# First mixer on x as it lands, with a third pair of output weights and zero products ahead; 106 filler instructions taken out

## The chip, the cores and the metric

One core of one Trainium2 chip runs the whole program. The metric is the device time of one execution in microseconds. The median over the runs shown is 1749.64 us for the kernel before.

## What is computed

The reference runs four layers over one sequence of 256 tokens with 1024 channels, all in float32: an even mixer, a retention mixer, a pool mixer and an MLA attention, each followed by a feed-forward part (a gated convolutional one in the first two layers, a mixture of 32 experts in the last two). The change is to the first, the even mixer:

```python
def rms_norm(x, g):
    y = xf * lax.rsqrt(jnp.mean(xf * xf, axis=-1, keepdims=True) + EPS)
    return (y * g).astype(x.dtype)

def even_mixer(xn, w_in, q_gain, k_gain, sconv_w, w_out):
    proj = xn @ w_in
    q, k, v, gate_b, gate_c, h = jnp.split(proj, ...)     # six parts of 512 columns
    q = rms_norm(heads(q), q_gain)
    k = rms_norm(heads(k), k_gain)
    a = dilated_attention(q, k, v)                        # 8 heads of 64
    b = gate_b * causal_dwconv(gate_c * h, sconv_w)
    return jnp.concatenate([a, b], axis=-1) @ w_out

x = x + even_mixer(rms_norm(x, even_norm[e]), ...)
```

## The kernel before

Each engine's instructions are written out in their own order (`@block.tensor`, `@block.scalar` and so on, L2582 on), and engines meet at semaphores, `E("name")`. TensorE is given products in three parts: a float32 operand is split into a high part (rounded, by ScalarE's copy into an fp32r tile) and a low part (the rest, by VectorE's subtraction), and `three_products` (L724) forms high x high, high x low and low x high.

**The even mixer's weights** come through a ring of six slots of 16 KB for each partition, and are split in 32 quarters of 128x1024 elements. Quarters 0 to 11 are of q, k and v, and are used with the turned x as the stationary operand (12 products of 512 columns each, L732 and L773). Quarters 12 to 23 (`Q_CONV` on) are gate_c, h and gate_b, four quarters each, formed in `conv_chunk` (L797) by channels. Quarters 24 to 31 (`Q_OUT` on) are the output weights (L835). `even_rounds` (L746, ScalarE, rounding at L754) and `even_rests` (L758, VectorE, L761) split them into one of two pairs of buffers, `e_w[q % 2]`; quarter q may be rounded once quarter q - 2 is used (`q_used`).

**The start.** SyncE loads both tiles of x (128 tokens each, L2562, L2563), then the first weight slab in four pieces of 512 KB (`quarter_in0` to 2 at L711, the fourth at L712). ScalarE's queue loads the constants with the identity and then the parameters (L2605, L2606). ScalarE squares x's tile 0 (L431), VectorE tile 1 (L477), GpSimd takes both means to the power -1/2 (`norm_pool`, L471), VectorE scales x into `hs` (L493), TensorE turns `hs` by products with the identity (`norm_pe`, L545), ScalarE evacuates the turned chunks times the norm's gain as high parts (L446) and VectorE makes their low parts (L505). Then `first_quarter` (L773) runs by chunk.

**Between.** ScalarE evacuates q and k (a square at L878, a copy at L879) and v. VectorE sums the squares of each head (L937), GpSimd takes 32 columns of means to the power (L906), VectorE scales q and k (L944), and only behind this come its `rests` for quarters 13 on. The gates are evacuated by ScalarE at L883 (gc) and L894 (gb); VectorE multiplies gc by h (L969), runs the short convolution, multiplies by gb (L981) and splits the result into `mix_hi` and `mix_lo` (L983, L984), which output quarter 28 needs. VectorE's split of the first feed-forward gate half (L1177) is in two parts around its last quarter.

**Filler.** `idle(b, n)` (L515) issues n products of the identity with itself, two instructions each, whose result nobody reads. They stand before the conv chunks (L808, 6), in the last head (L597, 5), before norms 1, 3 and 4 (`IDLE`, L520: 14, 7, 8), before the second slab of each feed-forward part (L1041, 5 twice) and before the MLA output projection (L1689, 5): 55 products, 110 instructions. The routing (L1904) has products of the same sort, which the diff doesn't touch.

Of the kernel before, what the change touches and what calls it, by code (L numbers as in the profile page):

```python
# [142 lines left out]
def build(nc, const, decay_in, band_in, params, rows, x_in, w_in, w_out, wq, wk, wv, wg, wo_r, w_up, w_down, pool_w, w_dkv, w_uk, w_uv,  # L143
# [6 lines left out]
    with ctx:  # L150
# [56 lines left out]
        def spread(col, *shape):  # L207
# [20 lines left out]

        qk_t = area(0, NT, 2 * BANK)
        v_t = area(2048, NT, BANK)  # L230
        qT, kT = area(3072, 4, S), area(14592, 2, 4, S)
        gbT, gcT, zT = area(5120, 4, S), area(6144, 4, S), area(7168, 4, S)
        mix_hi = placed("mix_hi", [P, 8, S], work_at + 4 * 8192, F32R)
# [8 lines left out]
               for i in range(2)]  # L242
        assert 3 * QUARTER <= n_rows and 12544 + QUARTER <= 13568
# [161 lines left out]
        RAW_X = (2,)  # L405

        def scaled_before(k):

            return NT * sum(j not in RAW_X for j in range(k))

        def norm_act(act, link, k, meanwhile=None):
# [23 lines left out]
            if meanwhile:  # L435
# [25 lines left out]
        def tiles(k):  # L461

            return (1, 0) if k == 0 else (0, 1)

        def norm_pool(pool, k):
            for i, t in enumerate(tiles(k)):
                if k == i == 0:
                    pool.wait_ge(E("ev_small"), 2)
                else:
                    pool.wait_ge(E("n_ms"), NT * k + i + 1)  # L470
                nc.gpsimd.tensor_tensor(rstd[:, t:t + 1], ms[:, t:t + 1], C("minus_half")[:, 0:1],  # L471
                                        ALU.pow).then_inc(E("n_rstd"), 1)

        def norm_dve(dve, link, k, meanwhile=None):
            if k == 0:
                dve.wait_ge(E("first_in"), 16 * (NT + 1))
                link(nc.vector.scalar_tensor_tensor(hs[:, 1, :], x[:, 1, :], 1.0 / D, x[:, 1, :], ALU.mult, ALU.mult, accum_out=ss[:, 1, 0:1]))  # L477
                nc.vector.tensor_scalar(ms[:, 1:2], ss[:, 1, 0:1], EPS, None, ALU.add).then_inc(E("ev_small"), 1)
# [5 lines left out]
            for i, t in enumerate(tiles(k)):  # L484
                if k in RAW_X:
                    break
# [7 lines left out]
            if meanwhile:  # L494
                meanwhile()
            g = G("g_kvin" if k == 6 else NORMS[k])
            if k in SPLIT:
                for b in range(4):
                    if k in RAW_X and b == 0:
# [15 lines left out]
        def idle(b, n):  # L515

            for _ in range(n):
                nc.tensor.matmul(bank(b, P), ident, ident, start=True, stop=True)

        IDLE = {1: (0, 14), 3: (0, 7), 4: (4, 8)}  # L520

        def norm_pe(pe, k):
            if k in IDLE:
                idle(*IDLE[k])
# [13 lines left out]
            for i, t in enumerate(tiles(k)):  # L538
                if k in RAW_X:
# [205 lines left out]

        def even_rounds(act, units, first, end):  # L746
            for q in range(first, end):
# [4 lines left out]
                if q >= 2:  # L752
                    act.wait_ge(E("q_used"), q - 1)
# [1972 lines left out]
```

## Time and profile before

| | us |
|---|---|
| the three runs | 1746.04, 1749.64, 1750.04 |
| median | 1749.64 |
| the profiled execution, whole | 1746.62 |
| its span, first to last instruction | 1744.8 |
| TensorE busy in it | 1698.7 (97%) |
| VectorE, ScalarE, GpSimd busy | 864.9, 488.8, 21.5 |

The profile is one execution. The page sums it up; the timeline lists an engine's instructions in order, those of one line together, with the idle time ahead of them and what ended it. A product's duration in the timeline includes the way through the array, so products that follow one another overlap: their pace is read from their starts.

### The profile page before, as it was taken

The page shows a single profiled execution, that of the slowest core. Times are in us where ns is not written, and L with a number is a line of the kernel's source. Part 1 is how long each engine was busy: PE and PEld are TensorE (multiplying, and loading weights), DVE is VectorE, ACT ScalarE, POOL GpSimd, SP SyncE. Part 2 cuts the span into 40 slices and gives each one's busy share as a digit, 9 for nine tenths or more (in the row PEclk, how much of TensorE's full clock was granted, in tenths as well). Part 3 has the DMA queues.
Part 4 walks back from the last instruction along what each step waited for, and adds up shares of the span by engine and source line. Part 5 has one row for each costly group of instructions (what it writes and reads, how often), then busy time and mean ns, then how long its engine had stood idle before and what let it go on. Part 6 is the DMA issues. An engine that isn't in the chain of part 4 may idle for free.

```text
span 1744.8 us, 23694 instructions
## 1 busy us (share of the span) xinstructions
PE 1698.7 (97%) x9686; PEld 1137.0 (65%) x9686; DVE 864.9 (50%) x1532; ACT 488.8 (28%) x747; POOL 21.5 (1%) x31
## 2 busy tenths in 40 slices
PE   7999999999999999999999999999999999999997
PEld 6979999987789999844444444447764444444343
DVE  5778777774668777623324233233652233233233
ACT  5555444444445444310100000013430000001001
POOL 0100000000000000000000000000000000000000
PEclk9999999999999999999999999999999999999998
DMA  9535556664509555899999999998479999999995
GB/s 371 197 116 174 173 188 225 193 200 150 197 24 314 180 181 221 321 363 423 426 425 424 429 425 425 421 418 317 159 304 406 427 425 425 426 424 427 426 420 245
DMA packets 120507, 542.42 MB, mean 311 GB/s; under 512 B 6104, under 2 KB 52320, under 8 KB 92128
## 3 DMA queue, kind: packets, MB, share of 16 engines
q1 hardware_dynamic: 119984, 539.75, 78.3%
q8 instruction: 65, 1.06, 0.2%
q10 hardware_dynamic: 432, 1.39, 0.2%
q14 instruction: 26, 0.21, 0.0%
HBM read 540.07 MB, written 1.05 MB: 310 GB/s over the span
## 4 chain that ended last, share of the span: by engine, by line
PE 88%; DVE 5%; DMA 5%; ACT 1%; issue 1%; POOL 0%; DVEq 0%; SPq 0%; ACTq 0%; POOLq 0%
PE PS L2109 23%; PE PS L2146 12%; PE PS L726 11%; PE PS L727 11%; PE PS L728 11%; PE PS L2061 6%; DMA ring<-w_up 4%; PE PS L567 2%; PE PS L2090 2%; PE PS L2091 1%; DVE e_w_lo L761 1%; PE PS L2127 1%; PE PS L1598 0%; PE PS L1052 0%; PE PS L1296 0%
## 5 line engine op out<-in xcount | busy, mean ns | idle before, releaser
L2109 PE MATMUL PS<-ring,work 128*64 128x512 f32 x1152 | 280.5, 593 | 4.6 <-DMA ring<-w_up 4.6
L2214 DVE SCALAR_TENSOR_TENSOR work<-PS,small,work 128x512 f32<-128x512 f32 x32 | 24.0, 751 | 454.1 <-PE PS L2109 454.1
L2109 PE MATMUL PS<-work 128*64 128x512 f32 x656 | 203.2, 592 | 0.0
L2109 PEld LDWEIGHTS PS<-ring,work 128*64 128x64 f32 x1152 | 91.3, 137 | 167.3 <-issue 166.5
L2146 PE MATMUL PS<-ring,work 128*64 128x512 f32 x576 | 155.9, 595 | 1.6 <-ACT work L2175 1.6
L2167 ACT ACTIVATE work<-PS 128x512 f32<-128x512 f32 x32 | 19.1, 597 | 403.5 <-PE PS L2109 403.5
L2109 PEld LDWEIGHTS PS<-work 128*64 128x64 f32 x656 | 66.2, 137 | 92.2 <-issue 91.9
L2061 PEld LDWEIGHTS PS<-work,hs 128*128 128x128 f32 x1024 | 120.6, 194 | 7.8 <-issue 3.2
L2061 PE MATMUL PS<-work,hs 128*128 128x128 f32 x1024 | 121.9, 278 | 1.8 <-DVE work L2044 1.8
L2146 PE MATMUL PS<-work 128*64 128x512 f32 x368 | 122.7, 605 | 0.7 <-ACT work L2175 0.7
L1272 DVE TENSOR_TENSOR r_w_lo<-ring,r_w_hi 128x1024 fp32r<-128x1024 f32 x64 | 78.0, 1224 | 59.3 <-ACT r_w_hi L1265 57.9
L2162 ACT ACTIVATE y_hi<-PS 128x512 fp32r<-128x512 f32 x62 | 37.0, 597 | 232.1 <-PE PS L2091 216.4
L2146 PEld LDWEIGHTS PS<-ring,work 128*64 128x64 f32 x576 | 48.7, 137 | 78.9 <-issue 77.7
L1265 ACT ACTIVATE r_w_hi<-ring 128x1024 fp32r<-128x1024 f32 x64 | 67.9, 1066 | 112.4 <-PE PS L728 106.9
L728 PE MATMUL PS<-f_x_hi,f_w_value_lo 128*128 128x256 f32 x352 | 98.8, 281 | 0.0
L726 PE MATMUL PS<-f_x_hi,f_w_value_hi 128*128 128x256 f32 x352 | 98.8, 281 | 0.0
L727 PE MATMUL PS<-f_x_lo,f_w_value_hi 128*128 128x256 f32 x352 | 98.8, 281 | 0.0
L2194 DVE TENSOR_TENSOR x_res<-x_res,PS 128x512 f32<-128x512 f32 x128 | 81.5, 679 | 22.3 <-PE PS L2091 22.3
L726 PE MATMUL PS<-f_x_hi,f_w_gate_hi 128*128 128x256 f32 x320 | 90.0, 281 | 1.3 <-DVE work L1203 1.3
L727 PE MATMUL PS<-f_x_lo,f_w_gate_hi 128*128 128x256 f32 x320 | 89.8, 281 | 0.0
L728 PE MATMUL PS<-f_x_hi,f_w_gate_lo 128*128 128x256 f32 x320 | 89.8, 281 | 0.0
L2188 DVE TENSOR_TENSOR y_lo<-PS,y_hi 128x512 fp32r<-128x512 f32 x62 | 42.9, 691 | 82.5 <-ACT y_hi L2162 82.5
(377 smaller groups left out, 3398.1 us busy)
## 6 DMA issues: line engine op xcount, KB each, us to landing
ring<-w_gate SPq DMA_DIRECT2D x28, 2048.0 KB, 26.8
ring<-w_up SPq DMA_DIRECT2D x28, 2048.0 KB, 26.1
ring<-w_down SPq DMA_DIRECT2D x26, 2048.0 KB, 24.7
ring<-ffn_w_up SPq DMA_DIRECT2D x22, 2048.0 KB, 8.7
work<-w_gate SPq DMA_DIRECT2D x16, 2048.0 KB, 31.1
work<-w_down SPq DMA_DIRECT2D x14, 2048.0 KB, 21.9
ring<-ffn_w_down SPq DMA_DIRECT2D x22, 1024.0 KB, 6.1
work<-w_up SPq DMA_DIRECT2D x10, 2048.0 KB, 22.7
```

The lines of the kernel that those rows point to most:

```text
L567: last = nc.tensor.matmul(dst, lhs(c), w(c), start=(c == 0), stop=(c == n - 1))
L726: nc.tensor.matmul(dst, lhs[0], rhs[0], start=start, stop=False, skip_group_check=True)
L727: nc.tensor.matmul(dst, lhs[0], rhs[1], start=False, stop=False, skip_group_check=True)
L728: return nc.tensor.matmul(dst, lhs[1], rhs[0], start=False, stop=stop, skip_group_check=True)
L1265: nc.scalar.activation(r_w[q % 3][0][:, :], raw_quarter(units, q), ACT.Copy).then_inc(E("q_round"), 1)
L1272: nc.vector.tensor_tensor(r_w[q % 3][1][:, :], raw_quarter(units, q), r_w[q % 3][0][:, :].bitcast(F32), ALU.subtract).then_inc(E("q_split" ...
L2061: last = nc.tensor.matmul(bank(GATHER[b])[:, c * P:(c + 1) * P], hs[:, t, (4 * b + c) * P:(4 * b + c + 1) * P], sel[:, t, :], start=(t == ...
L2109: last = nc.tensor.matmul(PS[CAP * e:CAP * (e + 1), what, :], xg[:, c, CAP * e:CAP * (e + 1)], chunk_of(w[e], c), start=(c == 0), stop=(c ...
L2146: last = nc.tensor.matmul(PS[CAP * e:CAP * (e + 1), 2 + n, :], e_hT[:, c, CAP * e:CAP * (e + 1)], part_of(w[e], c)[n], start=(c == 0), sto ...
L2162: nc.scalar.activation(hi[:, :], bank(2 + n), ACT.Copy).then_inc(q["y_hi"], 1)
L2188: nc.vector.tensor_tensor(lo[:, :], bank(2 + n), hi[:, :].bitcast(F32), ALU.subtract).then_inc(q["y_lo"], 1)
L2194: nc.vector.tensor_tensor(v, v, bank((banks or COMBINE[n])[t]), ALU.add).then_inc(q["add"], 1)
```

## The change

1. The first norm's factor is applied later. TensorE turns raw x. ScalarE squares both tiles between the roundings of quarters 4 and 5, GpSimd takes the power, and ScalarE's evacuations of q, k and v are scaled by `rstd`. For the gates, two products of `rstd` with the identity (four instructions, in place of the first six fillers) lay the factor out by token; ScalarE copies and squares it, and GpSimd multiplies gc by the square and gb by the factor, four products of 128x512 in place.
2. x's tile 1 is loaded on ScalarE's queue in place of the parameters, which SyncE loads behind the first weight piece. ScalarE rounds quarter 0 first, then evacuates four turned chunks, rounds quarter 1, and evacuates the other four; VectorE follows in the same order.
3. TensorE issues three products of a zeroed 128x512 tile (`blank`, six instructions) before it waits for x.
4. The output quarters have three pairs of buffers; from quarter 27 on rounding waits for quarter q - 3 instead of q - 2. The feed-forward gate half is rounded and split wholly behind quarter 31.
5. All `idle` calls go: 110 instructions out, four in for the layout of `rstd`, which makes 106.

```diff
+        blank = area(0, BANK)
+        token_rms, token_rms_2 = area(4096, S), area(4096 + S, S)
+        e_w += [[placed(f"e_w2_{part}", [P, QUARTER], work_at + 4 * (14592 + QUARTER * j), F32R) for j, part in enumerate(("hi", "lo"))]]
...
 def norm_act(act, link, k, meanwhile=None):
-            if k == 0:
-                act.wait_ge(E("first_in"), 16 * (NT + 1))
-                link(nc.scalar.activation(hs[:, 0, :], x[:, 0, :], ACT.Square, accum_out=ss[:, 0, 0:1]))
-                nc.scalar.activation(ms[:, 0:1], ss[:, 0, 0:1], ACT.Copy, bias=EPS, scale=1.0 / D).then_inc(E("n_ms"), NT)
...
             if k == 0:
+                meanwhile(1)
                 act.wait_ge(E("param_in"), 16)
             g = G(NORMS[k])
             for b in (range(4) if k == 6 or k in SPLIT else [1, 3]):
+                if k == 0 and b == 2:
+                    meanwhile(2)
                 act.wait_ge(E("n_tr"), 4 * k + b + 1)
...
 def norm_dve(dve, link, k, meanwhile=None):
-            if k == 0:
-                dve.wait_ge(E("first_in"), 16 * (NT + 1))
-                link(nc.vector.scalar_tensor_tensor(hs[:, 1, :], x[:, 1, :], 1.0 / D, x[:, 1, :], ALU.mult, ALU.mult, accum_out=ss[:, 1, 0:1]))
-                nc.vector.tensor_scalar(ms[:, 1:2], ss[:, 1, 0:1], EPS, None, ALU.add).then_inc(E("ev_small"), 1)
...
-        IDLE = {1: (0, 14), 3: (0, 7), 4: (4, 8)}
 def norm_pe(pe, k):
-            if k in IDLE:
-                idle(*IDLE[k])
...
-                                               chunk((x if k in RAW_X else hs)[:, t, :], k, c), ident)
+                                               chunk((x if k in UNSCALED else hs)[:, t, :], k, c), ident)
...
 def heads_pe(...)
-                    if kind == "ev" and h == 7:
-                        pe.wait_ge(E("at_sc"), 7)
-                        idle(4, 5)
...
 def even_load(sp, units)
                         sp.dma_start(view(units.slot(), DC, BANK)[:, 2 * k:2 * k + 2, :], src[:, 2 * k:2 * k + 2, :]).then_inc(E(f"quarter_in{k}"), 16)
+                        if k == 0:
+                            sp.dma_start(par[:, :], params).then_inc(E("param_in"), 16)
...
+        def even_place(q):
+            return e_w[q % 2 if q < Q_OUT else (q - Q_OUT) % 3]
...
-                    act.wait_ge(E("q_used"), q - 1)
+                    act.wait_ge(E("q_used"), q - 1 - (q > Q_OUT + 2))
...
 def even_pe(pe, units)
-            idle(0, 6)
+            pe.wait_ge(E("n_rstd"), NT)
+            for t in range(NT):
+                last = nc.tensor.matmul(bank(2)[:, t * P:(t + 1) * P], rstd[:, t:t + 1].to_broadcast([P, P]), ident, start=True, stop=True)
+            last.then_inc(E("tok_ps"), 1)
...
 def even_act(act, units, link)
             for n in range(3):
+                if n == 0:
+                    rounds(5)
+                    for t in range(NT):
+                        link(nc.scalar.activation(sq[t], x[:, t, :], ACT.Square, accum_out=ss[:, t, 0:1]))
+                        nc.scalar.activation(ms[:, t:t + 1], ss[:, t, 0:1], ACT.Copy, bias=EPS, scale=1.0 / D).then_inc(E("n_ms"), 1)
                 rounds(4 * n + 6)
+                if n == 0:
+                    act.wait_ge(E("n_rstd"), NT)
...
-                    nc.scalar.activation(dst, bank(4 + 2 * (n % 2) + t), ACT.Copy).then_inc(E("ev_qkv"), 1)
+                    nc.scalar.activation(dst, bank(4 + 2 * (n % 2) + t), ACT.Copy, scale=rstd[:, t:t + 1]).then_inc(E("ev_qkv"), 1)
+            act.wait_ge(E("tok_ps"), 1)
+            nc.scalar.activation(token_rms, bank(2, S), ACT.Copy).then_inc(E("ev_tok"), 1)
+            nc.scalar.activation(token_rms_2, bank(2, S), ACT.Square).then_inc(E("ev_tok"), 1)
...
-            rounds(Q_EVEN - 1)
-            units.n += 1
+            rounds(Q_EVEN)
             ffn_first_act(act, units, 0, GATE)
-            units.n -= 1
-            rounds(Q_EVEN)
...
 def even_pool(pool)
+            pool.wait_ge(E("ev_tok"), 2)
+            for i, (gates, by) in enumerate(((gcT, token_rms_2), (gbT, token_rms))):
+                for b in range(2):
+                    pool.wait_ge(E("ev_gc"), 2 * i + b + 1)
+                    v = gates[:, 2 * b:2 * b + 2, :]
+                    nc.gpsimd.tensor_tensor(v, v, by.unsqueeze(1).to_broadcast([P, 2, S]), ALU.mult).then_inc(E("ev_scaled"), 1)
...
 def ffn_pe(pe, units, l)
-                if isinstance(s, int) and s == 1:
-                    idle(0, 5)
...
             sp.dma_start(x[:, 0, :], x_in[0, 0:P, :]).then_inc(E("first_in"), 16)
-            sp.dma_start(x[:, 1, :], x_in[0, P:S, :]).then_inc(E("first_in"), 16)
...
 @block.tensor
+            pe.wait_ge(E("ev_small"), 1)
+            for _ in range(3):
+                nc.tensor.matmul(bank(7), blank[:, 0:P], blank, start=True, stop=True)
             pe.wait_ge(E("first_in"), 16 * (NT + 1))
...
 @block.scalar
-            act.dma_start(par[:, :], params).then_inc(E("param_in"), 16)
+            act.dma_start(x[:, 1, :], x_in[0, P:S, :]).then_inc(E("first_in"), 16)
...
 @block.vector
+            nc.vector.memset(blank, 0.0)
```

## Rows read from the trace of the kernel before

**Rows 1.** The page: TensorE's granted clock, in tenths, over 40 equal slices.

```profile
PEclk9999999999999999999999999999999999999998
```

**Rows 2.** Timeline 0 to 24 us: start, duration, engine, line, operation, tiles, count, [idle before, releaser].

```profile
7.07 1.06 ACT L431 ACTIVATE hs<-x_res 128x1024 f32<-128x1024 f32 x1 [3.90 <-DMA x_res<-x]
...
8.56 1.38 POOL L471 TENSOR_TENSOR small<-small,tables 128x1 f32<-128x1 f32 x2 [8.11 <-DVE small L478]
8.87 1.06 ACT L754 ACTIVATE e_w_hi<-ring 128x1024 fp32r<-128x1024 f32 x1 [0.35 <-DMA ring<-even_w_in]
...
10.05 3.65 PE L545 MATMUL PS<-tables,hs 128*128 128x128 f32 x16 [10.05 <-DVE hs L493]
...
12.52 3.03 ACT L446 ACTIVATE f_x_hi<-PS,tables 128x256 fp32r<-128x256 f32 x8 [1.25 <-PE PS L545]
...
13.35 0.78 PE L779 MATMUL PS<-e_w_hi,f_x_hi 128*128 128x512 f32 x1
...
16.70 0.39 PE L779 MATMUL PS<-e_w_hi,f_x_hi 128*128 128x512 f32 x1
```

**Rows 3.** Timeline around norm 1, TensorE and VectorE.

```profile
127.71 3.29 PE L518 MATMUL PS<-tables 128*128 128x128 f32 x28
...
130.44 0.75 DVE L493 TENSOR_SCALAR hs<-x_res,small 128x1024 f32<-128x1024 f32 x1 [0.44 <-POOL small L471]
...
134.02 3.23 DVE L505 SCALAR_TENSOR_TENSOR f_x_lo<-PS,tables,f_x_hi 128x256 fp32r<-128x256 f32 x8 [0.16 <-DVE f_w_value_lo L1169]
```

**Rows 4.** Timeline 19 to 30 us: a quarter's low part and TensorE's next quarter.

```profile
20.80 1.23 DVE L761 TENSOR_TENSOR e_w_lo<-ring,e_w_hi 128x1024 fp32r<-128x1024 f32 x1 [1.52 <-ACT e_w_hi L754]
...
22.22 0.39 PE L779 MATMUL PS<-e_w_hi,f_x_hi 128*128 128x512 f32 x1
```

**Rows 5.** DMA issues, 0 to 120 us: queue, count, KB each, median us to landing.

```profile
ring<-even_w_in SPq DMA_DIRECT2D x4, 512.0 KB, 8.3
...
x_res<-x SPq DMA_DIRECT2D x2, 512.0 KB, 4.7
...
tables<-params ACTq DMA_DIRECT2D x1, 509.5 KB, 6.3
```

**Rows 6.** Timeline, ScalarE: an evacuation, the rounding behind it, two scaled evacuations.

```profile
26.14 0.58 ACT L878 ACTIVATE work<-PS 128x512 f32<-128x512 f32 x1
...
28.05 1.08 ACT L754 ACTIVATE e_w_hi<-ring 128x1024 fp32r<-128x1024 f32 x1
...
62.86 1.26 ACT L887 ACTIVATE work<-PS,small 128x512 f32<-128x512 f32 x2
```

**Rows 7.** Timeline 42 to 53 us: GpSimd's power and TensorE's filler and wait.

```profile
44.67 5.44 POOL L906 TENSOR_TENSOR small<-small,tables 128x32 f32<-128x32 f32 x1 [34.73 <-DVE small L939]
...
47.53 1.50 PE L518 MATMUL PS<-tables 128*128 128x128 f32 x12
...
52.56 0.39 PE L726 MATMUL PS<-f_x_hi,e_w_hi 128*128 128x256 f32 x1 [0.67 <-DVE e_w_lo L761]
```

**Rows 8.** Timeline, ScalarE: the second gb gate.

```profile
102.70 0.59 ACT L894 ACTIVATE work<-PS 128x512 f32<-128x512 f32 x1
```

**Rows 9.** Timeline, TensorE in the output quarters: its two waits.

```profile
115.11 0.50 PE L726 MATMUL PS<-e_w_hi,mix_hi 128*128 128x512 f32 x1 [0.34 <-DVE e_w_lo L761]
...
123.50 0.50 PE L726 MATMUL PS<-e_w_hi,mix_hi 128*128 128x512 f32 x1 [1.25 <-DVE e_w_lo L761]
```

**Rows 10.** Timeline, TensorE: waits behind fillers, last head and norm 3.

```profile
101.73 0.55 PE L603 MATMUL PS<-tables,work 128*128 128x128 f32 x3 [1.46 <-DVE work L645]
...
522.15 1.05 PE L545 MATMUL PS<-tables,hs 128*128 128x128 f32 x7 [0.62 <-DVE hs L493]
```

**Rows 11.** Stretches: length, busy us (instructions) by engine, granted clock, DMA share, GB/s.

```profile
1096.00:1104.00 8.00, 5.70 (x28) 1.95 (x26) 0.00 (x0) 0.60 (x1) 0.00 (x0) 1.00 1.00 426
...
1724.60:1727.80 3.20, 3.20 (x10) 0.96 (x8) 0.00 (x0) 0.00 (x0) 0.00 (x0) 0.50 0.14 56
1728.00:1731.00 3.00, 3.00 (x16) 1.01 (x14) 0.00 (x0) 0.00 (x0) 0.00 (x0) 1.00 0.00 0
```

More of the change, by code:

```diff
@@ L404, in build @@
         SHARED = (1, 2, 3, 4)
-        RAW_X = (2,)
+        RAW_X, UNSCALED = (2,), (0, 2)
         def scaled_before(k):
-            return NT * sum(j not in RAW_X for j in range(k))
+            return NT * sum(j not in UNSCALED for j in range(k))
         def norm_act(act, link, k, meanwhile=None):
@@ L428, in norm_act @@
                                          scale=1.0 / D).then_inc(E("n_ms"), 1)
-            if k == 0:
-                act.wait_ge(E("first_in"), 16 * (NT + 1))
-                link(nc.scalar.activation(hs[:, 0, :], x[:, 0, :], ACT.Square, accum_out=ss[:, 0, 0:1]))
-                nc.scalar.activation(ms[:, 0:1], ss[:, 0, 0:1], ACT.Copy, bias=EPS, scale=1.0 / D).then_inc(E("n_ms"), NT)
             if k == 8:
                 return
-            if meanwhile:
+            if meanwhile and k:
                 meanwhile()
             if k == 0:
+                meanwhile(1)
                 act.wait_ge(E("param_in"), 16)
@@ L461, in tiles @@
         def tiles(k):
-            return (1, 0) if k == 0 else (0, 1)
+            return range(NT)
         def norm_pool(pool, k):
             for i, t in enumerate(tiles(k)):
[L467 to L470, printed above, removed]
+                pool.wait_ge(E("n_ms"), NT * k + i + 1)
                 nc.gpsimd.tensor_tensor(rstd[:, t:t + 1], ms[:, t:t + 1], C("minus_half")[:, 0:1],
@@ L484, in norm_dve @@
             for i, t in enumerate(tiles(k)):
-                if k in RAW_X:
+                if k in UNSCALED:
                     break
@@ L494, in norm_dve @@
             if meanwhile:
-                meanwhile()
+                meanwhile() if k else meanwhile(1)
             g = G("g_kvin" if k == 6 else NORMS[k])
@@ L498, in norm_dve @@
                 for b in range(4):
+                    if k == 0 and b == 2:
+                        meanwhile(2)
                     if k in RAW_X and b == 0:
@@ L513, in norm_dve @@
                                         spread(g[:, 2 * b:2 * b + 2], 2, S), ALU.mult).then_inc(E("n_xd"), 1)
-        def idle(b, n):
-            for _ in range(n):
-                nc.tensor.matmul(bank(b, P), ident, ident, start=True, stop=True)
-        IDLE = {1: (0, 14), 3: (0, 7), 4: (4, 8)}
         def norm_pe(pe, k):
-            if k in IDLE:
-                idle(*IDLE[k])
             if NORMS[k] == "g_pool":
@@ L538, in norm_pe @@
             for i, t in enumerate(tiles(k)):
-                if k in RAW_X:
+                if k in UNSCALED:
                     name, values = X_DONE[k]
@@ L770, in quarter @@
                 pe.wait_ge(E("q_split"), q + 1)
-                return [view(v[:, :], *shape) for v in e_w[q % 2]]
+                return [view(v[:, :], *shape) for v in even_place(q)]
             def first_quarter(w, k):
@@ L877, in even_act @@
                     if n < 2:
-                        nc.scalar.activation(sq[t][:, n * BANK:(n + 1) * BANK], bank(4 + 2 * n + t), ACT.Square)
-                    nc.scalar.activation(dst, bank(4 + 2 * (n % 2) + t), ACT.Copy).then_inc(E("ev_qkv"), 1)
+                        nc.scalar.activation(sq[t][:, n * BANK:(n + 1) * BANK], bank(4 + 2 * n + t), ACT.Square, scale=rstd[:, t:t + 1])
+                    nc.scalar.activation(dst, bank(4 + 2 * (n % 2) + t), ACT.Copy, scale=rstd[:, t:t + 1]).then_inc(E("ev_qkv"), 1)
+            act.wait_ge(E("tok_ps"), 1)
+            nc.scalar.activation(token_rms, bank(2, S), ACT.Copy).then_inc(E("ev_tok"), 1)
+            nc.scalar.activation(token_rms_2, bank(2, S), ACT.Square).then_inc(E("ev_tok"), 1)
             for b in range(2):
@@ L932, in even_dve @@
                 nc.vector.memset(kT[other, i, :, :], 0.0)
-            norm_dve(dve, link, 0, meanwhile)
+            norm_dve(dve, link, 0, rests)
+            nc.vector.tensor_tensor(gqk, G("q_gain"), G("k_gain"), ALU.mult).then_inc(E("ev_small"), 1)
             rests(10)
@@ L985, in even_dve @@
             dve.wait_ge(E("ev_conv"), 1)
-            rests(Q_EVEN - 1)
-            rest_part(dve, 0, GATE, 0, units.slot(1), 0)
             rests(Q_EVEN)
-            rest_part(dve, 0, GATE, 0, units.slot(), 1)
+            for part in range(2):
+                rest_part(dve, 0, GATE, 0, units.slot(), part)
             residual_dve(dve, "even", first_bank=4)
@@ L1308, in ret_pe @@
                                                     start=True, stop=True)
-                        last.then_inc(E("rt_tok_ps"), 1)
+                        last.then_inc(E("tok_ps"), 1)
                     continue
@@ L1446, in ret_dve @@
                     rests(4)
-                    dve.wait_ge(E("rt_tok_ps"), 1)
+                    dve.wait_ge(E("tok_ps"), 2)
                     for name in ("r_cos", "r_sin"):
@@ L1686, in project @@
             def project(h):
-                if h == 0:
-                    idle(4, 5)
                 pe.wait_ge(E("ml_lo"), h + 1)
```

22 lines of the change are left out of this document (9 added, 13 removed).

## The prediction

> **What bounds the kernel now.** I read the page first: its clock row stands at 9 in all 40 slices but the last [rows 1], so TensorE runs at its 2.4 GHz level nearly throughout, and the page has it busy for 97% of the span. So a gain can come only from what TensorE waits for or does for nothing. I then read the timeline of the first stage, by engine, and looked for TensorE's waits and for what ends them. Nearly everything the diff touches lies before 146 us; the rest of it is filler in later stages. Until 10.05 TensorE does nothing. x's second tile is there at about 7 us; ScalarE's square (7.07, with read and mean over by about 8.5) and two powers on GpSimd (from 8.56) come before the first transpose, which then runs slowly: 16 transposes in 3.65 us [rows 2] against 28 like-sized instructions in 3.29 us later [rows 3]. The first product is issued at 13.35, the first of quarter 1 at 16.70, of quarter 3 at 22.22 [rows 2, 4]: 5.52 us for two quarters, 2.76 each. From there to quarter 12 TensorE is the bound, with the pair of weight buffers close behind: a quarter's low part starts at 20.80 and takes 1.23, so it is there at 22.03 for a product at 22.22 [rows 4].
>
> **The start.** Squares, powers and scaling leave the path, since raw x is turned. What is late next? x's second tile now goes on ScalarE's queue beside the weights' first piece on SyncE's, and the parameters go behind that piece. Before, x took 4.7 us as a median of its two loads, the parameters 6.3, the weight pieces 8.3 [rows 5], and the first rounding at 8.87 waited for its piece [rows 2]. One 512 KB piece follows another by some 1.35 us (8.87 and 10.21 are the first two). I take x at 7.0, unchanged, piece 0 at 7.45 (one piece earlier), the parameters at 8.75 and piece 1 at 10.1 as before. Then: round quarter 0 7.45 to 8.5, its low part on VectorE to 9.8; ScalarE's turned halves from 8.8, eight in 3.03 us as now [rows 2], four before it breaks off. First product about 9.85, not 13.35. Quarter 1: round from 10.35, VectorE first does four low halves (0.40 each, [rows 3]: eight in 3.23), so its low part ends at 12.7: product at 12.75 against 16.70. Quarter 2 in the same way at 15.6 against 19.46 (16.70 + 2.76). Gain here **3.85**.
>
> The three wide zero products are issued from about 1.5 us, when `blank` is set, and at the lower clock last some 5.1 us (six instructions of twice 512 columns at 1.2 GHz), to 6.6: x isn't there yet, so they cost nothing. If they failed to raise the clock, the transposes would end at 7.0 + 3.65 = 10.65, and quarter 0's products would be slower by up to 1.6 (16.70 - 13.35 is 3.35 now against 2.76, so 0.6 is what the present one pays). From 0 to 1.6; I take 0, as 5 us of dense products precede, while before only 4.3 us of work lay ahead of the fast products.
>
> **What is given back.** The squares come back on ScalarE between the roundings of quarters 4 and 5. One takes 7.07 to about 8.5, so 1.45, two 2.9. ScalarE is free there for 2.76 - 1.06 = 1.7; the pair of buffers has 0.2 to spare [rows 4]. So TensorE waits 2.9 - 1.7 - 0.15 = **1.1** for quarter 5. The first evacuation of four now has a scale read from memory: four take 28.05 - 26.14 = 1.91 without one [rows 6]; the two scaled ones at 62.86 take 1.26 together, 0.57 apart, against 0.48: 0.35 more for four. Behind a delayed quarter 5, quarter 6 is late by some **0.4**, and the second evacuation delays quarter 10 and VectorE's sums by **0.35**. So 3.85 - 1.1 - 0.4 - 0.35 = **2.0** arrives at quarter 12.
>
> **Six fillers before the gate chunks** (12 instructions, 1.50 us at 47.53) [rows 7]. Removed, but TensorE then waits longer for quarter 13, which VectorE splits only after GpSimd's power of 32 columns (44.67, 5.44 us) and a product of its own; TensorE goes on at 52.56 after a wait of 0.67 [rows 7]. That chain starts from VectorE's sums and moves by 2.0, so **0** comes from this filler. The two new products (four instructions) lie in the same wait.
>
> **GpSimd's four products** of 128x512 (two gates, two halves) have no row. The nearest are its powers: 0.69 for one column, 5.44 for 32 [rows 2, 7]. By the column that would be 0.15 each and 80 us for 512; from below, VectorE's kind of time, some 0.7. A power isn't a product, so I take 1 to 2. The gc gates aren't wanted before 77.8 (evacuated by 63). The gb gates are evacuated by 103.3 [rows 8], and the chain to `mix_hi`, now from 108.82, must begin by about 110.1: cover for 6.8 us. Cost **0** under that. The Trainium skill's GPSIMD Engine Reference, section 3.1, gives 2.6 cycles an element for such an operation at 1.2 GHz, an estimate of 1.1 us, and the sum would be the same.
>
> **Third pair for the output weights.** TensorE waits 0.34 at 115.11 and 1.25 at 123.50 for a low part [rows 9]; with the drain of 0.17 each that those idle times don't count, 0.5 + 1.4 = 1.9. The condition before quarter 26 stays that quarter 24 is used, and from 27 on each may start a quarter earlier. Following it through: quarter 28's low part ends 114.5 for a product at 114.6, 29 to 31 have a microsecond and more. The gate half's low parts, now both behind quarter 31, end near 123.1, before the first sum at 123.75. Gain **1.9**.
>
> **Fillers in the other gaps.** Ahead of norm 1, 28 instructions run 127.71 to 131.00, and the first transpose at 130.84 follows without a wait [rows 3]. It could start at 130.0, but the second tile is scaled at 130.44 for 0.75, so the last transpose gains 0.5, and the low halves (until 137.25 [rows 3]) take back 0.3: **0.2**. Everywhere else TensorE waits after the filler: 1.46 after the heads, 0.62 before norm 3 [rows 10], 0.63 twice before the second slab, 0.16 before the pool, 0.74 in the projection: **0**.
>
> Without the clock: 2.0 + 1.9 + 0.2 = **4.1 us faster**.
>
> **The clock.** In the profile it falls in three stretches inside the work and once at the end. Where it stands at 0.50, TensorE issued 10 instructions in 3.20 us; just behind, at 1.00, 16 in 3.00 [rows 11]: about 1.6 us lost where it is the bound. What came before the falls: waits of 0.75 and 0.46 between short 32-column products near 734, of 0.74 and 1.36 near 1290, and transposes of eight rows before 1724, with hardly a wait. Not after the 2.30 wait for a load in 1096 to 1104, at 1.00 [rows 11]. So it isn't a wait's length alone, but how little is done. Without fillers seven waits grow: heads 2.6, norm 1 2.2, norm 3 2.2, second slabs 1.8 twice, pool 2.0, projection 1.9, each with little work about it. Bounds: none (the 2.30 row) to all seven (11.2 us). I take two falls at 1.5, some of it beside other waits: **3.0** lost. The skill's page TensorE: Matmul & The Clock Gate, in Why this matters for your kernels, asks only that no long idle gap stand between bursts, and all these would pass: by it, nothing is lost. The falls near 734 and 1724 don't agree with it, the row at 1096 does.
>
> **Sum.** The profiled execution took 1746.62 (span 1744.8 and 1.8 around it), 3.0 under the median of the three runs, 1749.64. 1746.6 - 4.1 + 3.0 = 1745.5 on its terms; against the median 1749.64 - 1.1 = **1748.5**.
>
> **The rivals.** (A) The forecast, the clock falls in one to three more places: 1747 to 1750. Chance 0.40.
> (B) The clock holds in all the gaps, as behind the 2.30 wait: 1749.6 - 4.1 = 1745.5, 1743 with a better start (x landing before 7.0, or no stall by the squares). 0.28. This is what the page's rule gives.
> (C) Slower: the clock falls at nearly all seven gaps, for the work there is too thin. 7 x 1.6 = 11.2, less 4.1: +7.1, 1756.7. It outweighs the gain from the third fall on, and is over 0.3% slower from the sixth. 0.12.
> (D) The change doesn't do what it says at the start: the first product is bound by loads and parameters, or the clock isn't raised by products of zeros; 1.6 and 0.5 less, with two falls: 1750.6. 0.14.
> (E) GpSimd's product on the gb gates takes over 6.8 us; each microsecond more delays `mix_hi` by one. At 10 us, 1751.7 with the falls. 0.06.
>
> **How the numbers follow.** 0.3% of 1749.6 is 5.2 us, about what a measurement can tell from no change: faster is under 1744.4, slower over 1754.9. Faster: most of B's better half and some of the spread between runs (4 us in three), 0.24. Slower: C and a tail of E, 0.14. The rest, 0.62, is within. The range leaves out B's best and C's worst: 1743.0 to 1755.5.
>
> **What would show it.** Right: first product near 9.9; a wait of about 1 us for quarter 5; quarter 13 at about 50.5, after a wait near 1.6; no wait in the output quarters; the last of them issued near 123.6; clock at 0.50 in one to three new stretches behind former fillers. Wrong: clock 1.00 in all (B) or down in most (C); a first product after 11; GpSimd products over 6 us.

## The result, and the profile after

The changed kernel takes 1754.10 us (median of 8 runs, 1747.43 to 1757.16), the kernel before 1747.60 beside it (8 runs). The ratio is 1.0029, 95% interval 1.0016 to 1.0041: slower, by some 5 us. The profiled execution took 1753.27, its span 1751.5. What the change does itself came out near the forecast or a little better; what it gave up cost three times what I had put down. Of the 13 executions of the last kernel in the table of experiments below, one took 3339.44 us, near twice the rest; it is left out there, and it is the one that was profiled.

**The start and the third pair.** Timeline of the changed kernel, 0 to 10 us, columns as in [rows 2]:

```profile
1.47 5.20 PE L2584 MATMUL PS<-work 128*128 128x512 f32 x6 [1.47 <-DVE small L2651]
7.13 2.01 PE L533 MATMUL PS<-tables,x_res 128*128 128x128 f32 x16 [0.46 <-DMA x_res<-x]
7.42 1.06 ACT L745 ACTIVATE e_w_hi<-ring 128x1024 fp32r<-128x1024 f32 x1 [4.24 <-DMA ring<-even_w_in]
8.51 1.23 DVE L752 TENSOR_TENSOR e_w_lo<-ring,e_w_hi 128x1024 fp32r<-128x1024 f32 x1 [4.75 <-ACT e_w_hi L745]
8.81 1.57 ACT L448 ACTIVATE f_x_hi<-PS,tables 128x256 fp32r<-128x256 f32 x4 [0.33 <-DMA tables<-params]
9.79 0.50 PE L770 MATMUL PS<-e_w_hi,f_x_hi 128*128 128x512 f32 x1 [0.64 <-DVE e_w_lo L752]
```

The products of zeros end at 6.67, ahead of x; the transposes take 2.01 us, where they took 3.65; the first product is at 9.79, where it was at 13.35, and what ends its wait is the low part of the weights. The squares then cost a wait before the sixth quarter (quarter 5, counted from 0), and GpSimd's products are short. Rows of the timeline: that quarter, the last head, and the transposes of norm 1:

```profile
24.44 0.50 PE L713 MATMUL PS<-e_w_hi,f_x_hi 128*128 128x512 f32 x1 [0.44 <-DVE e_w_lo L752]
...
99.24 0.55 PE L588 MATMUL PS<-tables,work 128*128 128x128 f32 x3 [2.56 <-DVE work L630]
...
125.58 3.68 PE L533 MATMUL PS<-tables,hs 128*128 128x128 f32 x16 [2.18 <-DVE hs L488]
```

And GpSimd's four products among the groups of lines (busy us, mean ns of one; idle before them and its releasers):

```profile
L913 POOL TENSOR_TENSOR work<-work 128x512 f32<-128x512 f32 x4 | 6.2, 1546 | 48.3 <-ACT work L898 37.2 <-ACT work L887 11.1
```

Landmarks in the two profiles, in us from the start of the span, say where the time went. The gain is 4.5 us at the last output quarter and 4.6 at norm 3; then it melts, and between the two expert layers alone 8.4 us are lost.

| TensorE's first | before | after | difference |
|---|---|---|---|
| product of quarter 0 | 13.35 | 9.79 | -3.56 |
| instruction behind quarter 11 | 47.53 | 45.14 | -2.39 |
| product of quarter 12 | 48.78 | 45.51 | -3.27 |
| output product | 103.54 | 101.04 | -2.50 |
| product of the last output chunk | 127.48 | 123.01 | -4.47 |
| feed-forward product | 132.75 | 128.91 | -3.84 |
| transpose of norm 3 | 522.15 | 517.57 | -4.58 |
| one-hot product of routing 0 | 732.37 | 730.59 | -1.78 |
| expert product, layer 0 | 741.35 | 741.42 | +0.07 |
| expert product, layer 1 | 1296.52 | 1304.95 | +8.43 |
| end of the span | 1744.83 | 1751.48 | +6.65 |

**The clock.** Stretches of the changed kernel (length; busy us and instructions of TensorE, its weight loads, VectorE, ScalarE, GpSimd; granted clock; DMA share; GB/s):

```profile
123.00:132.00 9.00, 6.82 (x44) 6.43 (x43) 8.01 (x14) 6.34 (x14) 1.15 (x2) 0.81 0.42 125
518.00:522.00 4.00, 4.00 (x24) 3.87 (x22) 3.50 (x4) 3.54 (x8) 0.00 (x0) 0.57 0.10 20
709.00:713.00 4.00, 3.62 (x17) 3.62 (x18) 0.81 (x2) 0.28 (x1) 0.55 (x1) 0.57 1.02 398
1102.00:1105.00 3.00, 2.84 (x8) 1.11 (x10) 0.00 (x0) 0.00 (x0) 0.00 (x0) 0.50 1.01 431
1184.00:1187.00 3.00, 2.48 (x7) 1.92 (x8) 1.13 (x3) 2.43 (x11) 0.00 (x0) 0.50 1.06 426
1248.00:1252.00 4.00, 3.77 (x10) 2.94 (x11) 2.88 (x8) 0.98 (x4) 0.00 (x0) 0.59 0.17 68
1297.00:1303.00 6.00, 5.68 (x27) 5.38 (x26) 3.40 (x22) 0.00 (x0) 0.00 (x0) 0.50 1.00 427
```

It falls to its 1.2 GHz level as TensorE starts again at norm 1 (the 16 transposes at 125.58 take 3.68 us), norm 3, the pool and the output projection: four of the seven places that lost their filler. It falls also at 1101.9, at 1183.8, and at 733 and 1297 it stays down for longer than before. Before, it fell near 734, 1291 and 1724, and at the end. The fall at 1101.9 isn't bound to a missing filler: two kernels below that have their fillers show it too, at 1103.8 and 1099.1.

**A wait that nobody had asked for.** Timeline of the changed kernel, the transposes of raw x behind the first expert layer:

```profile
1179.99 1.60 PE L1859 MATMUL PS<-tables,x_res 128*128 128x128 f32 x12 [0.58 <-DVE x_res L2192]
1184.52 1.12 PE L1859 MATMUL PS<-tables,x_res 128*128 128x128 f32 x4 [2.92 <-issue]
```

Twelve of the 16 run, then TensorE stands for 2.92 us with "issue" as the reason: nothing in the profile holds it. In the trace a block of instructions is loaded on queue 8 within this wait; of 1180 to 1184 the DMA view has

```profile
q8 instruction: 1, 0.02, 1.7%
```

The kernel before has no such wait there, though it has such a load too: the DMA view of its 1178 to 1182 has the same line, and its 16 transposes run from 1178.03 without a break. So the load alone doesn't explain the wait. What is special about the place is that just ahead of these transposes TensorE's instructions jump past a block that isn't needed (`moe_pe_more`, products for experts that are given more tokens than fit).

### The profile page after: what moved, and what is told of

Its sections match the earlier page's. It is cut to its first block, busy times and chain, and to the rows that moved or that the text cites. A ratio compares the mean times of both kernels' runs of the same rounds, so it can differ in the third digit from the quotient of the medians.

```text
span 1751.5 us, 23500 instructions
## 1 busy us (share of the span) xinstructions
PE 1699.9 (97%) x9586; PEld 1133.4 (65%) x9586; DVE 862.0 (49%) x1528; ACT 491.1 (28%) x752; POOL 27.3 (2%) x35
## 4 chain that ended last, share of the span: by engine, by line
PE 88%; DMA 5%; DVE 5%; ACT 2%; issue 1%; POOL 0%; DVEq 0%; SPq 0%; ACTq 0%
PE PS L2107 23%; PE PS L2144 12%; PE PS L713 11%; PE PS L714 11%; PE PS L715 11%; PE PS L2059 6%; DMA ring<-w_up 4%; PE PS L555 2%; PE PS L2088 2%; PE PS L2089 1%; PE PS L2125 1%; DVE e_w_lo L752 1%; PE PS L1598 1%; PE PS L1052 0%; PE PS L1296 0%
```

## The experiments

Each was timed in turn with the kernel before, in three sets; the median of the kernel before lay between 1747.6 and 1749.2, its mean at 1748.0, 1748.0 and 1748.6 in the three, so kernels of different sets compare to some tenths of a microsecond. Beside the median stands the time at the low clock level per run: twice the span times what the mean granted clock lacks of 1. In the profiles 4.4 to 6.7 us of it are at the end; the start isn't in it, since ahead of the first rise the profile shows no low level. Means are given where kernels are compared with each other; their standard errors are 0.5 to 1.2 us (0.2 for the kernel before). "All fillers" means all but the six before the gate chunks, which stay out (98 instructions of the 110).

| kernel | runs | median us | mean us | us at the low level | ratio to before, 95% |
|---|---|---|---|---|---|
| before | 86 | 1748.5 | 1748.2 | 21 | |
| changed | 8 | 1754.1 | 1753.4 | 40 | 1.0029 [1.0016, 1.0041] |
| changed, all fillers | 5 | 1743.3 | 1743.2 | 19 | 0.9968 [0.9955, 0.9981] |
| the same again | 12 | 1743.4 | 1743.3 | 19 | 0.9969 [0.9957, 0.9980] |
| changed, fillers at norms | 11 | 1745.2 | 1744.9 | 22 | 0.9979 [0.9966, 0.9993] |
| changed, the other fillers | 11 | 1747.4 | 1746.6 | 29 | 0.9992 [0.9978, 1.0006] |
| before, no fillers | 5 | 1757.2 | 1757.8 | 32 | 1.0055 [1.0042, 1.0068] |
| changed, 60 idle instructions | 12 | 1749.4 | 1749.8 | 37 | 1.0010 [1.0000, 1.0021] |
| changed, wide fillers | 12 | 1744.1 | 1743.8 | 22 | 0.9978 [0.9970, 0.9987] |
| all fillers, two pairs | 12 | 1745.4 | 1745.8 | 21 | 0.9987 [0.9978, 0.9996] |
| all fillers, no zeros | 12 | 1744.0 | 1744.1 | 19 | 0.9979 [0.9969, 0.9989] |
| all fillers, longer busy products | 12 | 1744.3 | 1743.7 | 18 | 0.9975 [0.9963, 0.9986] |
| the same, four products of zeros | 12 | 1742.7 | 1743.0 | 16 | 0.9967 [0.9955, 0.9978] |

**1. The fillers put back, all and in two halves, and taken from the kernel before.** The theory: the change's own parts gain about 4 us, and the clock takes more than that back where the fillers are gone. The rival: the loss has nothing to do with the fillers.

The cut shows the norms' part, with `IDLE = {1: (0, 14), 3: (0, 7), 4: (4, 8)}`, and one of the others (heads, second slabs, projection):

```diff
 def norm_pe(pe, k)
+            if k in IDLE:
+                idle(*IDLE[k])
...
 def heads_pe(...)
+                    if kind == "ev" and h == 7:
+                        pe.wait_ge(E("at_sc"), 7)
+                        idle(4, 5)
...
```

> The kernel after with all fillers put back but the six before the gate chunks (98 instructions, in the same seven places and counts as before the change). Theory 1 (the even block gained its 4.5 us and the clock took it back in the gaps that lost their filler): no stretch of 0.50 before the routing of the first expert layer, landmarks stay 4 to 5 us ahead of before up to there, and the time comes out 3.5 to 4.5 us under before, about 1743.5. Theory 2 (the later loss has nothing to do with the fillers: the earlier arrival falls badly on the loads or on the routing stages): still 3 to 7 us over before.

> The kernel before with nothing changed but all 110 filler instructions taken out. Theory 1: new stretches of 0.50 behind norm 1, norm 3, the pool and the MLA projection, in some runs behind the last head and the second slabs too; each costs about 1.6 us, so 6 to 10 us over before, 1754 to 1757. Theory 2: within 1 us of before, or a little faster (0.2 by norm 1).

> The kernel after with fillers only before norms 1, 3 and 4 (28, 14 and 16 instructions). Theory 1: norm 1, norm 3 and the pool, which fell in the profile of after (three of its new stretches), hold; that is worth 3 to 5 us against after, so about level with before or 1 to 2 us faster. Theory 2: as after.

> The kernel after with fillers only in the last head, before both second slabs and before the MLA projection (10 instructions each, 40). Theory 1: the projection's fall goes, norm 1, norm 3 and the pool stay low, so 1 to 3 us under after, still 2 to 4 over before. Theory 2: as after.

With all of them the changed kernel takes 1743.3 us (17 runs), 5.0 us under the kernel before by the means. So the whole loss is in what was given up: 10.1 us (1753.4 - 1743.3). The norms' fillers bring 8.5 of it back (1744.9) where I expected 3 to 5, the others 6.8 (1746.6) where I expected 1 to 3. That is more than 10.1 together, so something that either set removes is counted in both. A part of it is clock: the time at the low level goes from 40 us to 22 with the one set and to 29 with the other. The kernel before without its fillers loses 9.6 us as well, as expected, and its trace shows the other part:

```profile
1184.83 3.57 PE L1860 MATMUL PS<-tables,x_res 128*128 128x128 f32 x16 [4.86 <-issue]
```

The two kernels without any filler wait with reason "issue" behind the first expert layer, 2.92 and 4.86 us; the three kernels with fillers, few or many, don't.

One thing that I expected of the kernel before without fillers isn't in its profile: the clock holds at norm 1, norm 3, the pool and the projection, behind the same waits of 2.18, 2.18, 1.95 and 1.85 us. Of the places that lost their filler it falls at the last head alone (102.7), behind a wait of 2.60. Its norm 3, as a row of the timeline and as a stretch, to be read beside the stretch 518 to 522 above:

```profile
523.27 2.35 PE L544 MATMUL PS<-tables,hs 128*128 128x128 f32 x16 [2.18 <-DVE hs L493]
523.00:527.00 4.00, 3.67 (x28) 3.33 (x29) 3.19 (x3) 3.74 (x7) 0.62 (x1) 1.00 0.14 27
```

So the length of the wait doesn't settle whether the clock falls behind it. What does, no run here shows.

**2. The place of the code against the clock.** A filler product is four instructions in TensorE's stream (two products, each with a load of its stationary operand), so taking it out also moves all later code. To part the two: 120 waits for a semaphore that is long up, two to an instruction by my count, so 60 instructions, as many as fifteen fillers, and no product.

```diff
                 nc.tensor.matmul(bank(7), blank[:, 0:P], blank, start=True, stop=True)
+            for _ in range(120):
+                pe.wait_ge(E("ev_small"), 1)
```

> The changed kernel with 60 more instructions in TensorE's queue and no product more: waits for a semaphore that has been up since 1.5 us, put behind the three warm-up products and ahead of the wait for x, where TensorE is idle anyway. They put all later code of the engine 60 instructions further on, as far as the five products at the attention heads and the ten at the slabs do up to the first expert layer (each is four instructions). Theory of the place of the code: the 2.92 us at 1181.6, in the middle of the transposes behind the first expert layer, come from where a block of TensorE's instructions ends against the jump over the skipped branch; here, as in the kernel with those fillers, that wait is gone or under 0.5 us, the clock does not fall at 1183.8 for it, and the time is 3 to 4.5 us under that of the changed kernel: 1749.0 to 1750.5. The other clock falls of the changed kernel (125.7, 518.2, 709.4, 1101.9) stay. Rival, the missing products themselves (a clock that is low or about to fall when the branch is reached): the wait of about 3 us is still there and the time is that of the changed kernel, 1752.5 to 1754.

The timeline of this kernel at the same transposes:

```profile
1181.37 2.04 PE L1859 MATMUL PS<-tables,x_res 128*128 128x128 f32 x16 [0.60 <-DVE x_res L2192]
```

The wait is gone, and the fall of the clock with it (1.00 from 1184 to 1187, where it was 0.50). The time is 3.6 us less (standard error 1.4), as expected, and the falls at norm 1, norm 3 and the pool (127.6, 520.1, 711.3) stay. One thing in my expectation was false, that the 60 instructions lie beside idle time. Timeline of their kernel:

```profile
1.47 4.43 PE L2584 MATMUL PS<-work 128*128 128x512 f32 x6 [1.47 <-DVE small L2653]
8.10 3.61 PE L533 MATMUL PS<-tables,x_res 128*128 128x128 f32 x16 [2.20 <-issue]
11.40 0.54 PE L770 MATMUL PS<-e_w_hi,f_x_hi 128*128 128x512 f32 x1
```

x was there at 6.9, yet the transposes start at 8.10 and, the clock having fallen in the meantime, at half speed; the first product comes 1.6 us late. So the place of the code may cost more than the comparison shows.

**3. The same fillers in a third of the instructions.** Identity products of 512 columns, 16 instructions of the program for 49.

```diff
-                nc.tensor.matmul(bank(b, P), ident, ident, start=True, stop=True)
+            for _ in range((n + 3) // 4):
+                nc.tensor.matmul(bank(b, 4, P), ident, ident.unsqueeze(1).to_broadcast([P, 4, P]), start=True, stop=True)
```

> The changed kernel with fillers at the seven places again, but wide: products of the identity with itself four times side by side (512 columns), 16 instructions of the program in place of the 49 that the kernel with all fillers has. If what the fillers give is the clock alone, this gives the same: the two or three low stretches of the kernel with all fillers, 1743 to 1745 (some of the wide ones are longer than the wait that they lie in, by up to 0.7 us each at five places of them on the path, so not below 1743). If the count of instructions decides by itself where the code lies at the jump, a wait of 2 to 5 us at the transposes behind the first expert layer can show here in spite of the fillers, and then 1746 to 1749.

1743.8 us, with the falls at norm 1, norm 3, the pool and the projection gone and no "issue" wait: it is the products, not the number of instructions, that hold the clock.

**4. Two parts of the change undone, fillers kept.**

```diff
-            return e_w[q % 2 if q < Q_OUT else (q - Q_OUT) % 3]
+            return e_w[q % 2]
-                    act.wait_ge(E("q_used"), q - 1 - (q > Q_OUT + 2))
+                    act.wait_ge(E("q_used"), q - 1)
```

> The changed kernel with all fillers of the kernel before, and the third pair of weights for the output quarters taken back (quarters go through two pairs again, and the rounding waits one quarter earlier). By the prediction's own term the waits of 0.34 and 1.25 us at the output quarters come back, so the last output quarter starts 1.6 to 1.9 us later and the time is 1.9 us above the kernel with all fillers (1743.3): about 1745.2. Rival: the gain of the third pair is absorbed by what follows (the wait for the residual and the norm behind the last output product, or the feed-forward layer's first weights), and the time is within 0.6 us of 1743.3.

The waits are back. Timeline of TensorE in the output quarters of this kernel, to be read beside [rows 9]:

```profile
114.57 0.50 PE L725 MATMUL PS<-e_w_hi,mix_hi 128*128 128x512 f32 x1 [0.34 <-DVE e_w_lo L764]
...
122.76 0.50 PE L725 MATMUL PS<-e_w_hi,mix_hi 128*128 128x512 f32 x1 [1.03 <-DVE e_w_lo L764]
```

From the first output product to the last it takes 23.74 us against 21.96 with three pairs, 1.78 more; the time is 2.5 us more by the means (standard error 0.8). The pair's 1.9 us arrive at the end.

```diff
-            pe.wait_ge(E("ev_small"), 1)
-            for _ in range(3):
-                nc.tensor.matmul(bank(7), blank[:, 0:P], blank, start=True, stop=True)
```

> The changed kernel with all fillers of the kernel before, but without the three products of zeros at the start. Theory: the products of zeros are what has the clock granted at 6.2 us. Without them the 16 transposes run at half clock as before (3.65 us in place of 2.01), the first product starts at 7.13 + 3.3 = 10.4 us in place of 9.79, the second quarter at about 13.8 in place of 12.67; the wait of 0.44 us ahead of the sixth quarter takes up a part, and the time is 0.6 to 1.1 us above that of the kernel with all fillers (1743.3). Rival: the clock comes at the same time because the transposes alone raise it, and nothing changes (within 0.3 us at the second quarter).

```profile
7.00 3.65 PE L542 MATMUL PS<-tables,x_res 128*128 128x128 f32 x16 [7.00 <-DMA x_res<-x]
10.30 0.77 PE L782 MATMUL PS<-e_w_hi,f_x_hi 128*128 128x512 f32 x1
...
13.96 0.40 PE L782 MATMUL PS<-e_w_hi,f_x_hi 128*128 128x512 f32 x1
```

Without the zeros the transposes are slow again and the second quarter is at 13.96, where it is at 12.67 with them. The time is 0.8 us more (standard error 0.7): as expected, though the timing alone could not show it.

**5. Can the falls that are left be bought off?** In all profiles so far the clock falls near 730, and in all but the first of the kernel with all fillers also near 1290. These are the routings, where TensorE waits up to 0.75 and 1.37 us in spite of busy products of the kernel's own. (My expectation says that it falls at both places in every kernel; that one profile I had overlooked.)

```diff
-        FILLERS = (24, 10)
+        FILLERS = (29, 20)
```

> The changed kernel with all fillers of the kernel before once more, line for line, so that the two edits beside it are compared on the same chip and the gain of the change with its fillers kept rests on more runs. Theory that the change's own parts are worth what the traces show (start, third pair) once the clock and the place of the code are as before: 1743 to 1744, 0.2 to 0.3% under the kernel before. If 1743.3 was a lucky few runs: 1745 or more.

> The kernel with all fillers, and the kernel's own busy products in the two routings made longer, 24 to 29 ahead of the second half of the choice and 10 to 20 behind it (0.12 us each): in every kernel so far, with fillers or without, TensorE waits there 0.75 and 1.35 us for VectorE, and the clock falls at 725 to 735 and at 1288 to 1296. If a fall costs 1.3 us wherever it comes on TensorE's path, two falls fewer give 2.6 us: 1740.5 to 1742. Rival: the waits there are for VectorE's chain of one-hot rows, so half of what the clock costs is hidden by the next transfers of expert weights (TensorE waits for them 2.3 us at a time later in the layer), and the gain is under 1 us, 1742.5 to 1743.5. Longer by more than the wait, it would cost up to 0.2 us at each place.

> As the kernel beside it with the longer busy products, and four products of zeros at the start in place of three. In two profiles so far x landed at 8.1 us in place of 7.1, the products of zeros had ended 2.2 us before, and the clock fell at 8.1 (the second quarter 2.0 us later than in the others, of which 1.0 is x itself). If such a start is common, the fourth product (0.9 us at full clock, ending at about 6.8 to 7.6) is worth 1 us in those executions and costs up to 0.4 us where x is early: between -0.5 and +0.3 us on the median, so not to be told apart by the time, but by the profile: no low stretch at 8 us, and the transposes in 2.0 us whenever x lands.

The edit did what it was to do in its place. Timeline of the kernel with the longer busy products, and then a stretch of it:

```profile
725.47 5.90 PE L1918 MATMUL PS<-once 128*128 128x256 f32 x29
...
735.04 3.84 PE L2075 MATMUL PS<-work,hs 128*128 128x128 f32 x32 [0.16 <-DVE work L2058]
```

```profile
724.00:728.00 4.00, 4.00 (x20) 4.00 (x21) 2.03 (x11) 3.98 (x3) 0.00 (x0) 0.50 0.97 397
```

The wait before the gathering products is 0.16 us where it was 1.37. There is no fall near 1290 in this profile, but neither was there one in the first profile of the kernel without the edit. And in the first routing the clock is down already at 723.6, ahead of both waits, among the routing's own products of 36 columns (in the repeat without the edit from 723.1, and again at 733.3), and over all its runs the kernel has 18 us at the low level against 19. The time is 1743.7 against 1743.3: no gain, as the rival had it, though not for its reason; the falls weren't fewer. The fourth product of zeros, with 1743.0, can't be told from the others by its time either, and its profile can't be used, so that question stays open. (Its expectation names two profiles in which x landed at 8.1. There is one, of the kernel with two pairs; in the kernel with 60 idle instructions x had landed at 6.9.)

## Why the prediction was wrong

I forecast 1748.5 us, 1.1 under the kernel before; it was 1754.1, some 5 us over it. That this lies in my range is no merit: the range reached so far only for rivals C and E. The forecast was two opposite terms, 4.1 us of gain and 3.0 of clock. The gain was right; the clock was put far too low, and a third term was missing.

- **The start, 3.85 at the first quarters.** Right. First product 9.79 (forecast 9.85), second quarter 12.67 (12.75), third 15.54 (15.6). The order in which transfers land, and each engine's durations from rows of before, gave these within 0.1 us.
- **What is given back, 1.85.** A little high: 1.5. The gain is 3.9 at the third quarter and 2.39 at the end of quarter 11 (forecast 2.0). The wait for quarter 5 is 0.44 us, 0.6 with the drain (forecast 1.1): the two squares held ScalarE for 2.55 us (19.54 to 22.09), not 2.9. Those for quarters 6 and 10 are 0.22 and 0.37. That the first product of quarter 12 has gained 3.27 is the filler gone ahead of it, and TensorE waits longer for quarter 13 instead, as forecast: that came at 50.12 after a wait of 1.53 (50.5, near 1.6), 2.44 earlier.
- **GpSimd's products, 1 to 2 us.** Right: 1.55 us each. The estimate of 1.1 us from the Trainium skill's GPSIMD Engine Reference, section 3.1, was low by some 30%. No wait came of them: the first output product has gained 2.50, and the limit there is the last head.
- **The third pair, 1.9.** Right: 1.78 by undoing it, and no wait in the output quarters; last of them at 123.01 (123.6).
- **Norm 1, 0.2, and the other fillers, 0 without the clock.** This can't be seen apart: where the filler went, the clock fell with it.
- **The own parts together, 4.1.** 5.0 by the means with all fillers kept (1748.2 - 1743.3), 4.2 when both are taken at the same time at the low level (21 us against 19).
- **The clock, 3.0.** The step that failed. I priced a fall somewhat high and counted far too few. The lengths of the seven waits were right (2.56, 2.18, 2.18, 1.74 twice, 1.95 and 1.85 us); what follows from them wasn't. The price: I took half of the low stretch as lost, by rows 11. Over all 12 kernels, executions of one kernel differ by 0.37 us for each us at the low level (the regression within kernels, standard error 0.014), and TensorE does in 1 us there what takes it half a us, so about a quarter of the loss is hidden. The count: 40 us at the low level against 19 with the fillers, 7.6 us of time. I took two falls of the seven places; in the trace there were four, which by my own list meant "down in most", a sign of being wrong. Others came at 1101.9 and 1183.8, and the falls at 733 and 1297, which lie behind no filler, became longer. I had let the one row behind a wait of 2.30 us at 1.00 [rows 11] be my lower bound; in the changed kernel the wait for the same load was 2.83 us, and behind it, from 1102, the clock is at 0.50. One place in one execution doesn't say what happens there in the next, as the kernel before without fillers shows with the same four waits and no fall. And one of my rows was misread: the wait of 0.46 us near 734 stands at 737.22, behind the fall at 734.6, and not ahead of it.
- **What I didn't price at all: where the code lies.** 2.92 us in the trace; 2.5 us of the 10.1 are left when the clock's 7.6 are taken out. For six of the seven places I had put the removed fillers at 0 beyond the clock.

The sum from the runs: -4.2 for the own parts, +0.37 x 19 = 7.0 for the clock (40 us against 21 before), +2.5 for the instruction wait: +5.3, measured +5.2. This sum closes by construction, for the first and the last term are what the clock's price leaves over. What tests the price is that the remainders agree with the traces. These are the means less 0.37 us for each us at the low level (standard errors 0.1 to 0.6):

| kernel | mean without the clock's part, us | to the kernel that heads its group | what the traces show |
|---|---|---|---|
| changed, all fillers | 1736.1 | | |
| changed | 1738.6 | +2.5 | wait of 2.92 with "issue" |
| changed, 60 idle instructions | 1736.2 | +0.1 | wait gone, start up to 1.6 late |
| all fillers, two pairs | 1737.9 | +1.8 | output quarters 1.78 longer |
| all fillers, no zeros | 1736.9 | +0.8 | second quarter 1.3 later |
| before | 1740.3 | | |
| before, no fillers | 1745.8 | +5.5 | wait of 4.86 with "issue" |

Only the late start of the kernel with 60 idle instructions doesn't show in its remainder. The waits stand in one profile of each kernel, the means in all of its runs.

Rival C, "the clock falls at nearly all seven gaps", was nearest in size (+7.1) and in mechanism, though not in count; I gave it 0.12. B, the clock holds everywhere, is what the Trainium skill's page TensorE: Matmul & The Clock Gate (Why this matters for your kernels) would give, since to avoid drops it asks only that no long idle gap stand between bursts. The measurement decides against it for the changed kernel: the clock fell behind waits of 2.18 us (norm 1) and 1.95 us (pool) in its trace. In the trace of the kernel before without fillers it held behind both.

## What to carry to other kernels

Products that compute nothing, put into waits of about 2 us, were worth 10 us here, some 7.6 by the clock and 2.5 by where the later code lies: count them as part of the critical path before deleting them, and judge a place by whether the clock fell in other executions too, not in the one profiled. When a change has a cheap part that could undo a good one (here fillers out, start and buffers in), time the parts apart: the good part alone is 0.3% faster, the whole is 0.3% slower. And when the trace gives "issue" as the reason of a wait near a block of code that is jumped over, move the code by some dozen instructions before looking for a cause in the data.

## What the runs showed of the hardware

- TensorE stood 2.92 and 4.86 us with "issue" as the reason just behind a jump past an unused block of its instructions, in the two kernels without fillers; 60 more instructions at the start of its stream removed the wait. That it waited for its own instructions, and that the jump makes their loading late, is only argued: a load of a block stands on queue 8 within the wait, but one stands at this place in kernels without the wait as well.
- The clock need not do the same behind the same wait. At norm 1, norm 3 and the pool (waits of 2.18, 2.18 and 1.95 us) it fell in the profiles of the changed kernel, of that with 60 idle instructions and of that with the other fillers only, and held in that of the kernel before without fillers. Runs of one kernel have between 7 and 31 us at the low level (the kernel before).
- Waits for a semaphore that is already up are not free: 60 such instructions (by my count), issued from 1.5 us on behind three products, held the transposes until 8.10, so they took at most 0.11 us each (6.63 us for 60). The products ended at 5.90, x landed at 6.9, and no load of instructions stands in the trace between 0 and 20 us.
- Products of zeros raise the clock as others do: behind six of them from 1.47 us the transposes ran in 2.01 us, without them in 3.65. If x lands late, the gain is lost: with 6.8 us to its landing in place of 5.8 (the kernel with two pairs), the transposes took 3.61 us.
- Shortening the waits of the routings, near which the clock used to fall, left the time at the low level as it was (18 us against 19). It also falls among the routing's products of 36 columns, where TensorE doesn't wait (at 723.6 and 723.1 in two profiles).
